# One adaLN block more in the gated mixer, unread products in TensorE's gaps, and jumps moved ahead of the last waits

## The chip, the cores and the metric

The kernel runs on one core of a Trainium2 chip. The metric is the device time of one execution in microseconds, as the median of the runs. A core has TensorE (PE in the profile, its weight loads are PEld), VectorE (DVE), ScalarE (ACT), GpSimd (POOL) and SyncE (SP). All of them take their instructions in order and wait on semaphores; DMAs go out from the queues of SP and ACT.

## The reference, cut to what matters

One inference step of a four-layer trunk for 128 context tokens and 128 latent tokens (D = 1024), everything in float32. Layer i has a token mixer and then a channel mixer (a mixture of experts):

```
for i in range(4):
    mod = silu(cond) @ w_ada[i] + b_ada[i]            # 6 x 1024: sh1, sc1, g1, sh2, sc2, g2
    h = rmsnorm(x, norm_g[i, 0]) * (1 + sc1) + sh1
    y = (hyena_mixer, gla_mixer, fnet_mixer, pool_mixer)[i](h)
    x = x + g1 * y
    h = rmsnorm(x, norm_g[i, 1]) * (1 + sc2) + sh2
    x = x + g2 * hier_moe(h, ...)                     # 16 experts, top 1 group of 4, top 2 in it
y = rmsnorm(x, final_g)
```

The shifts, scales and gates (adaLN) depend on the conditioning vectors alone, so that they can be computed at any time before they are read. `gla_mixer` is the gated linear attention (projections wq, wk, wv, wg, two chunked scans, wo); `pool_mixer` takes window means and multiplies each of four groups of channels by a 256 x 256 matrix. All weights are read once: 552 MB in all.

## The kernel before, in words

**The weight stream.** Nearly all weights come through one ring of 14 slots of 1 MB (128 partitions x 2048 floats; `RING`, `SLAB`). `piece_stream()` writes the whole order of the pieces down by hand (L119 to L146), and SP walks it: for each piece it waits until the piece that had the slot 14 places before has been multiplied, and issues the DMA (L468; the experts' pieces mostly two at a time, L459). TensorE takes the pieces in the same order. `before[i]` is what stands ahead of the experts of layer i; an expert pair has 12 pieces (three matrices of four), and a layer has 8 pairs. The four pieces of the first pair's third matrix do not use the ring but lie in the arena (`first_w2`, L427), issued ahead of the layer's other experts.

**The adaLN blocks.** w_ada is cut into 12 blocks of 8 pieces, three blocks a layer. `ada(n, lo, hi)` on TensorE (L636 to L646; the products' line is L643) multiplies pieces lo to hi - 1 of block n by the conditioning; each piece is four products in four column groups of the array. When all 8 are done, DVE copies the sums out (`ada_rows(n)`, L1391), TensorE transposes them in four products (`ada_turned(n)`, L651), and DVE adds the bias (`ada_mod(n)`, L1399, L1404), which raises `mod_ready`. Block n + 1 may begin only after that. The code spreads the blocks by hand: blocks 0 to 4 in and behind the first mixer, 5, 6 and 7 in the gated mixer, 8 behind it and in the layer's router, 9 and 10 in the third layer, and 11 in the pool mixer.

**The gated mixer** is `pe_gla`. Around the change TensorE does block 6 (L523), the four pieces of wv (L531), `ada_turned(6)`, the second gate projection (L622), and the tiles of wg (L683) among the scans.

**The pool mixer** is at the end of TensorE's program: `ada(11, 0, 2)`, `norm(6)` (L657, the sums of squares, on ACT's squares from L1108), `ada(11, 2, 5)`, the products with pool_w (L1061), which ACT copies out (L1356), `ada(11, 5, 8)`, the window means (L1068), `ada_turned(11)`, and `norm(7)`.

**The router and the experts** are `moe(i, beside)`. TensorE multiplies the router's weights and transposes h (L860, L865), subtracts the rounded half of h (L875), and, after DVE has ranked the tokens (L1528 to L1543), counts them (L881 to L885). In layers 0 to 2 pieces of the adaLN block `beside` stand between these steps; in layer 3 nothing does. Then the first tokens are gathered (L702), and the pairs begin: L737 (first and second matrix), L761 (third), L720 (scatter).

**The start.** Two small products of the implicit filter (L910, L915), `norm(0)`, the filter's third layer (L925), and its spectrum (L906), with block 0 between them. ACT issues four small DMAs first (L1097 to L1100).

**The end.** After the last norm DVE writes eight tiles of the output (L1817), each raising `out_ready`. SP stores tiles 0 to 3 after the fourth, ACT tiles 4 to 7 after the eighth; SP waits for the stores and then runs `far_rounds`. That function jumps over code for experts with more tokens than 64 (further rounds, which these inputs do not need) to the end of the program: in the code its first instruction is the jump.

Of the kernel before, what the change touches and what calls it, by code (L numbers as in the profile page):

```python
# [21 lines left out]
P = 128  # L22
# [14 lines left out]
ADAS = 3 * LAYERS  # L37
# [81 lines left out]
def piece_stream():  # L119
# [4 lines left out]
    def pieces(name, count):  # L124
# [3 lines left out]
              ada(5, 0, 5) + pieces("wq", 2) + ada(5, 5) + pieces("wk", 2) + ada(6) + pieces("wv", 4)  # L128
              + pieces("wg", 4) + ada(7) + pieces("wo", 4) + ada(8),
              ada(9) + pieces("fn", 4) + ada(10),  # L130
              ada(11, 0, 5) + pieces("pool", 1) + ada(11, 5)]
# [31 lines left out]
def build(nc, a):  # L163
# [21 lines left out]
    with ctx:  # L185
# [218 lines left out]
        def _(sp):  # L404
# [65 lines left out]
            sp.wait_ge(s("out_ready"), 4)  # L470
            sp.dma_start(a["y"][:, 0:4], hT[:, 0:4]).then_inc(s("stored"), 16)
            sp.wait_ge(s("state_stored"), 32)
            sp.wait_ge(s("stored"), 16 * 2)

# [14 lines left out]
            far_rounds(sp, "sp", reg, one_round)  # L489

# [6 lines left out]
        def pe_gla(pe, arrived, ada, ada_turned, norm, h_ready, project, residual):  # L497
# [26 lines left out]
            for c in range(4):  # L524
                w8 = arrived(("wv", c), KD)
# [9 lines left out]
            ada_turned(6)  # L535
# [3 lines left out]
            def g_tiles(first, end):  # L539

                pe.wait_ge(s("mod_ready"), 7)
# [60 lines left out]
            ada(7, 0, 3)  # L602
# [9 lines left out]
            ada(7, 3, 8)  # L612
            residual(1, "wo", oT, lambda k: pe.wait_ge(s("o_ready"), k + 1), turned=7, beside=8)
# [12 lines left out]
        def _(pe):  # L626
# [227 lines left out]

            def moe(i, beside=None):
                pe.wait_ge(s("rw_loaded"), 16 * (i + 1))
                for k in range(KD):
# [19 lines left out]
                if beside is not None:  # L877
                    ada(beside, 6, 7)
                pe.wait_ge(s("members"), i + 1)
# [6 lines left out]
                if beside is not None:  # L886
                    ada(beside, 7, 8)
                pe.wait_ge(s("htok_rest"), 4 * (i + 1))
# [19 lines left out]

            pe.wait_ge(s("filter_loaded"), 16)
            mm(bank[5][0:HY_HID, 0:L], fsmall[0:HY_EMB, 1, 0:HY_HID], fsmall[0:HY_EMB, 0, :]).then_inc(s("f_mm"), 1)  # L910
            pe.wait_ge(s("cond_ready"), 3)
# [5 lines left out]
            last.then_inc(s("f_mm"), 1)  # L917
            norm(0)
# [94 lines left out]
            moe(1, 8)  # L1013


            ada(9, 0, 2)
            norm(4)
            ada(9, 2, 5)
# [14 lines left out]
            ada(9, 5, 8)  # L1033
# [9 lines left out]
            ada_turned(9)  # L1043
            pe.wait_ge(s("mix_rows"), 8 + 4)
            residual(2, "fn", rhs=fnm, beside=10)
            moe(2, 10)
# [37 lines left out]
        def _(act):  # L1084
# [150 lines left out]
            for c in range(10):  # L1235
                spectrum(c)
# [691 lines left out]
```

## Time and profile before

| what | value |
|---|---|
| median of 3 runs (lowest, highest) | 1424.62 us (1424.25, 1424.86) |
| profiled execution, its own time | 1424.48 us |
| its span, first to last instruction | 1422.3 us |
| time outside the span | 2.2 us |
| PE busy | 1358.9 us (96%) |
| PEld, DVE, ACT, POOL busy | 748.3, 360.7, 281.8, 32.1 us |
| chain that ended last, by engine | PE 83%, DMA 13%, DVE 2%, ACT 1% |
| read from HBM | 548.98 MB, 387 GB/s over the span |
| mean granted clock of TensorE | 0.992 of 2.4 GHz |

Read the table with two resources in mind: TensorE is busy nearly all the time, and so are the DMA engines; neither alone fills the span, so that each stage has its own bound.

### The profile page before, as it was taken

Reading aid. Unit: us, or ns where it says so; the run is one execution under the profiler, and the core shown is the slowest. Engines: PE = TensorE matmul, PEld = TensorE weight load, DVE = VectorE, ACT = ScalarE, POOL = GpSimd, SP = SyncE. Lnnn points to the kernel's source line nnn. Section 1 sums busy time; section 2 is a strip of 40 time slices with the busy share of each in tenths; the row PEclk is TensorE's granted clock in tenths of the full one; section 3 lists DMA queues with packets and bytes.
Section 4 is the critical chain, followed back from the end, with each engine's and each line's share of the span. In section 5 each row is a group of like instructions: output and inputs, shape, how many; then the busy total and the mean of one; then the engine's idle time right before and its main releaser. Section 6 shows DMA issues by size and latency. Waiting matters only on the chain.

```text
span 1422.3 us, 17398 instructions
## 1 busy us (share of the span) xinstructions
PE 1358.9 (96%) x7294; PEld 748.3 (53%) x7294; DVE 360.7 (25%) x881; ACT 281.8 (20%) x511; POOL 32.1 (2%) x30
## 2 busy tenths in 40 slices
PE   7999999999989999999999989999998898999986
PEld 3786585444435788774444436744443365444433
DVE  3434514111113303323111112331111153111113
ACT  3211024111103221232111104421111053111101
POOL 0001310000000000010000000100000000000000
PEclk9999999999999999999999999999999997999999
DMA  9955999999999993499999999999999999999993
GB/s 382 420 191 214 403 416 394 428 426 428 428 425 421 421 376 102 172 413 403 429 428 426 429 423 420 421 426 428 427 427 428 424 421 425 426 428 428 427 426 153
DMA packets 55076, 552.27 MB, mean 388 GB/s; under 512 B 6033, under 2 KB 8017, under 8 KB 8913
## 3 DMA queue, kind: packets, MB, share of 16 engines
q1 hardware_dynamic: 53360, 549.09, 92.5%
q10 hardware_dynamic: 1634, 2.01, 0.4%
q8 instruction: 60, 0.98, 0.3%
q14 instruction: 22, 0.18, 0.0%
HBM read 548.98 MB, written 2.10 MB: 387 GB/s over the span
## 4 chain that ended last, share of the span: by engine, by line
PE 83%; DMA 13%; DVE 2%; ACT 1%; SPq 0%; issue 0%; POOL 0%; DVEq 0%; POOLq 0%
PE bank L737 26%; PE bank L683 14%; PE bank L761 13%; DMA ring<-in_moe_w 10%; PE bank L643 5%; PE bank L702 5%; PE bank L720 3%; PE bank L514 2%; PE bank L531 2%; DMA ring<-in_pool_w 2%; PE bank L657 2%; PE bank L968 1%; PE bank L860 1%; PE bank L593 1%; PE bank L589 1%; PE bank L744 1%
## 5 line engine op out<-in xcount | busy, mean ns | idle before, releaser
L737 PE MATMUL bank<-ring,arena 128*64 128x512 f32 x896 | 200.4, 595 | 28.1 <-DMA ring<-in_moe_w 26.5
L737 PE MATMUL bank<-ring,hT 128*64 128x512 f32 x1024 | 225.3, 594 | 0.0
L761 PE MATMUL bank<-ring,arena 128*64 128x512 f32 x896 | 198.7, 596 | 0.6 <-DMA ring<-in_moe_w 0.6
L737 PEld LDWEIGHTS bank<-ring,arena 128*64 128x64 f32 x896 | 63.7, 137 | 157.6 <-issue 131.5
L737 PEld LDWEIGHTS bank<-ring,hT 128*64 128x64 f32 x1024 | 72.1, 137 | 139.4 <-issue 137.3
L1447 DVE TENSOR_TENSOR rows<-rows,bank 128x512 f32<-128x512 f32 x32 | 22.0, 688 | 463.6 <-PE bank L737 463.6
L761 PEld LDWEIGHTS bank<-ring,arena 128*64 128x64 f32 x896 | 61.6, 137 | 117.8 <-issue 114.6
L683 PE MATMUL bank<-hT,ring 128*128 128x256 f32 x512 | 112.4, 380 | 0.0
L683 PEld LDWEIGHTS bank<-hT,ring 128*128 128x128 f32 x512 | 96.5, 190 | 15.2 <-issue 2.5
L1167 ACT ACTIVATE yv_big<-bank,arena 128x512 fp32r<-128x512 f32 x64 | 44.0, 688 | 285.5 <-PE bank L761 285.5
L1466 DVE SCALAR_TENSOR_TENSOR yv_rest<-bank,arena,yv_big 128x512 fp32r<-128x512 f32 x64 | 48.1, 751 | 200.6 <-ACT yv_big L1167 200.6
L643 PE MATMUL bank<-ring,condT 128*32 128x512 f32 x768 | 91.1, 602 | 6.6 <-DMA ring<-in_w_ada 4.9
L683 PE MATMUL bank<-arena,ring 128*128 128x256 f32 x384 | 83.8, 380 | 1.2 <-DVE arena L1659 0.9
L683 PEld LDWEIGHTS bank<-arena,ring 128*128 128x128 f32 x384 | 72.6, 190 | 12.2 <-DVE arena L1659 1.2
L702 PE MATMUL bank<-sel,htok_big 128*128 128x256 f32 x256 | 69.8, 306 | 1.7 <-DVE sel L1434 1.7
L720 PE MATMUL bank<-selT,yv_big 128*128 128x256 f32 x256 | 66.7, 297 | 1.7 <-DVE yv_rest L1466 1.7
L702 PE MATMUL bank<-sel,htok_rest 128*128 128x256 f32 x256 | 65.0, 287 | 0.0
L720 PEld LDWEIGHTS bank<-selT,yv_big 128*128 128x128 f32 x256 | 48.0, 187 | 28.5 <-issue 26.0
L702 PEld LDWEIGHTS bank<-sel,htok_big 128*128 128x128 f32 x256 | 49.8, 195 | 23.9 <-issue 20.7
L720 PE MATMUL bank<-selT,yv_rest 128*128 128x256 f32 x256 | 62.2, 279 | 0.0
L1160 ACT ACTIVATE rows<-bank 128x512 f32<-128x512 f32 x32 | 19.1, 598 | 209.4 <-PE bank L737 209.4
L1150 ACT ACTIVATE arena<-bank 128x512 f32<-128x512 f32 x32 | 19.1, 598 | 158.0 <-PE bank L702 158.0
(217 smaller groups left out, 1281.7 us busy)
## 6 DMA issues: line engine op xcount, KB each, us to landing
ring<-in_moe_w SPq DMA_DIRECT2D x152, 2048.0 KB, 20.4
ring<-in_w_ada SPq DMA_DIRECT2D x96, 1024.0 KB, 22.0
ring<-in_moe_w SPq DMA_DIRECT2D x48, 1024.0 KB, 26.8
arena<-in_moe_w SPq DMA_DIRECT2D x16, 1024.0 KB, 19.6
arena<-in_moe_w SPq DMA_DIRECT2D x8, 2048.0 KB, 11.8
ring<-in_hy_w_in SPq DMA_DIRECT2D x12, 1024.0 KB, 27.3
ring<-in_hy_w_out SPq DMA_DIRECT2D x4, 1024.0 KB, 12.3
ring<-in_gla_w_v SPq DMA_DIRECT2D x4, 1024.0 KB, 22.8
```

Of the source, the lines that this page charges most:

```text
L514: last = mm(half(4 * w + h), w8[:, k, (h % 2) * P:(h % 2) * P + P], hT[:, k].rearrange("p g t -> p (g t)"), start=k == 0, stop=k == KD - 1)
L531: last = mm(bank[b][:, 256 * (c % 2):256 * (c % 2) + 256], hT[:, k, g], w8[:, k, :], start=k == 0, stop=k == KD - 1)
L643: last = mm(ada_bank(n)[32 * j:32 * j + 32, :], condT[:, G * k:G * k + 32], w[:, j, :], start=k == 0, stop=k == KD - 1)
L657: ins = mm(bank[6][:, 0:NT], ones[:], hT[:, k].rearrange("p g t -> p (g t)"), start=k == 0, stop=k == KD - 1)
L683: last = mm(dst, w[:, k, (m % 2) * P:(m % 2) * P + P], (hT[:, k] if rhs is None else rhs[:, k]).rearrange("p g t -> p (g t)"), start=k == ...
L702: last = mm(bank[b][:, (k % 2) * NT:(k % 2) * NT + NT], htok[n % 2][:, n // 2, k * P:k * P + P], sel[:, n // 2].rearrange("p e j n -> p (e ...
L720: last = mm(half(m), part[:, m * P:m * P + P], selT[:], start=first_pair and m % 2 == 0 and part is yv[0], stop=False, skip_group_check=True)
L737: last = mm(bank[4 + kind][SLOTS * e:SLOTS * e + SLOTS, :], x[:, k, at:at + SLOTS], w[:, kk, e, :], start=k == 0, stop=k == KD - 1)
L761: last = mm(bank[6 + q // 2][SLOTS * e:SLOTS * e + SLOTS, :], hidT[:, f, SLOTS * e:SLOTS * e + SLOTS], w[:, ff, e, :], start=f == 0, stop= ...
L1167: act_fn(yv[0][:, 512 * h:512 * h + 512], bank[6 + h][:], ACT.Identity, scale=wcol) \
L1447: tt(sil[:], sil[:], bank[5][:], ALU.mult).then_inc(s(pre + "hid_ready"), 1)
L1466: stt(yv[1][:, cols], bank[6 + h][:], wcol, yv[0][:, cols].bitcast(F32), ALU.mult, ALU.subtract) \
```

## The change

The order of the stream and of TensorE's blocks: layer 1 takes block 7 between the second and the third piece of wv, and blocks 8 and 9 where 7 and 8 were; layer 2 takes 10 and 11; layer 3 none. DVE's calls follow. `keep_running(n, x, b)` multiplies ones by x into a bank and nobody reads it; `wide_ones` is a column of ones repeated 512 times. Three of ACT's first DMAs are issued after the first norm. The output goes in four stores instead of two, and `far_rounds` comes ahead of the last waits on SP and ACT.

```diff
     before = [ada(0) + pieces("w_in", 12) + ada(1) + ada(2) + ada(3) + pieces("w_out", 4) + ada(4),
-              ada(5, 0, 5) + pieces("wq", 2) + ada(5, 5) + pieces("wk", 2) + ada(6) + pieces("wv", 4)
-              + pieces("wg", 4) + ada(7) + pieces("wo", 4) + ada(8),
-              ada(9) + pieces("fn", 4) + ada(10),
-              ada(11, 0, 5) + pieces("pool", 1) + ada(11, 5)]
+              ada(5, 0, 5) + pieces("wq", 2) + ada(5, 5) + pieces("wk", 2) + ada(6) + pieces("wv", 2) + ada(7)
+              + pieces("wv", 4)[2:] + pieces("wg", 4) + ada(8) + pieces("wo", 4) + ada(9),
+              ada(10) + pieces("fn", 4) + ada(11),
+              pieces("pool", 1)]
...
-            sp.wait_ge(s("out_ready"), 4)
-            sp.dma_start(a["y"][:, 0:4], hT[:, 0:4]).then_inc(s("stored"), 16)
-            sp.wait_ge(s("state_stored"), 32)
-            sp.wait_ge(s("stored"), 16 * 2)
...
             far_rounds(sp, "sp", reg, one_round)
+            sp.wait_ge(s("state_stored"), 32)
+            for k in (0, 4):
+                sp.wait_ge(s("out_ready"), k + 2)
+                sp.dma_start(a["y"][:, k:k + 2], hT[:, k:k + 2]).then_inc(s("stored"), 16)
+            sp.wait_ge(s("stored"), 16 * 4)
...
             for c in range(4):
+                if c == 1:
+                    ada_turned(6)
+                if c == 2:
+                    ada(7, 0, 8)
                 w8 = arrived(("wv", c), KD)
...
-            ada_turned(6)
+            ada_turned(7)
             gates(pe, 1)
...
-                pe.wait_ge(s("mod_ready"), 7)
+                pe.wait_ge(s("mod_ready"), 8)
...
-            ada(7, 0, 3)
+            ada(8, 0, 3)
...
-            ada(7, 3, 8)
-            residual(1, "wo", oT, lambda k: pe.wait_ge(s("o_ready"), k + 1), turned=7, beside=8)
+            ada(8, 3, 8)
+            residual(1, "wo", oT, lambda k: pe.wait_ge(s("o_ready"), k + 1), turned=8, beside=9)
...
+            wide_ones = ones[:, 0:1].broadcast_to([P, 512])
+            def keep_running(times, x, b=7):
+                for _ in range(times):
+                    mm(bank[b][:, 0:x.shape[1]], ones[:], x)
...
             def moe(i, beside=None):
                 pe.wait_ge(s("rw_loaded"), 16 * (i + 1))
+                if beside is None:
+                    pe.wait_ge(s("mod_ready"), ADAS)
+                    keep_running(2, wide_ones)
...
                 if beside is not None:
                     ada(beside, 6, 7)
+                else:
+                    keep_running(3, wide_ones)
                 pe.wait_ge(s("members"), i + 1)
...
                 if beside is not None:
                     ada(beside, 7, 8)
+                else:
+                    keep_running(1, wide_ones)
...
+            pe.wait_ge(s("cond_ready"), 1)
+            keep_running(2, ones[:], 0)
             pe.wait_ge(s("filter_loaded"), 16)
             mm(bank[5][0:HY_HID, 0:L], ...).then_inc(s("f_mm"), 1)
+            keep_running(12, ones[:], 0)
...
             last.then_inc(s("f_mm"), 1)
+            keep_running(3, ones[:], 0)
             norm(0)
...
-            ada(11, 0, 2)
             norm(6)
-            ada(11, 2, 5)
+            keep_running(2, wide_ones)
             pw = arrived(("pool", 0), KD)
...
-            ada(11, 5, 8)
             pe.wait_ge(s("mix_rows"), 12 + 4)
...
-            ada_turned(11)
             norm(7)
             moe(3)
...
-            act.dma_start(base[:], a["c_base"]).then_inc(s("base_loaded"), 16)
-            act.dma_start(ar(19472, 3 * P), a["c_masks"]).then_inc(s("masks_loaded"), 16)
             act.dma_start(skip_row[0:1], a["skip"]).then_inc(s("skip_loaded"), 16)
-            act.dma_start(rw[:], a["router"][0]).then_inc(s("rw_loaded"), 16)
...
             inverse_root(0)
+            act.dma_start(base[:], a["c_base"]).then_inc(s("base_loaded"), 16)
+            act.dma_start(ar(19472, 3 * P), a["c_masks"]).then_inc(s("masks_loaded"), 16)
+            act.dma_start(rw[:], a["router"][0]).then_inc(s("rw_loaded"), 16)
...
-            act.wait_ge(s("out_ready"), 8)
-            act.dma_start(a["y"][:, 4:8], hT[:, 4:8]).then_inc(s("stored"), 16)
             far_rounds(act, "act", reg, one_round)
+            for k in (2, 6):
+                act.wait_ge(s("out_ready"), k + 2)
+                act.dma_start(a["y"][:, k:k + 2], hT[:, k:k + 2]).then_inc(s("stored"), 16)
...
-            ada_rows(6)
-            ada_mod(6)
+            for n in (6, 7):
+                ada_rows(n)
+                ada_mod(n)
```

The other lines of the diff put 10 for 9, 11 for 10 and so on in the third layer, and take block 11's calls out of DVE's pool mixer.

## Rows read from the trace of the kernel before

**Rows 1.** The page's second part: what the DMAs moved in 40 slices of 35.6 us

```profile
GB/s 382 420 191 214 403 416 394 428 426 428 428 425 421 421 376 102 172 413 403 429 428 426 429 423 420 421 426 428 427 427 428 424 421 425 426 428 428 427 426 153
```

**Rows 2.** Windows: stretch, length, busy time (instructions) by engine, clock, DMA share, GB/s

```profile
524.00:590.00 66.00, 64.62 (x388) 57.08 (x387) 21.92 (x35) 17.77 (x26) 0.00 (x0) 1.00 0.30 108
1240.00:1329.00 89.00, 89.00 (x460) 37.64 (x456) 14.99 (x24) 10.89 (x17) 0.00 (x0) 1.00 1.01 428
```

**Rows 3.** TensorE's waits from 1326 to 1407 us: total, times, longest

```profile
PE bank L737 <- DMA ring<-in_moe_w: 7.5, 6, 1.3
```

**Rows 4.** The gated mixer: chain of waits, then SP's issues and their landing

```profile
488.59 7.00 PE bank L643 x64
495.59 27.82 PE bank L531 x128
...
469.73 3.07 SPq L468 DMA_DIRECT2D ring<-in_gla_w_v  x4
...
ring<-in_gla_w_v SPq DMA_DIRECT2D x4, 1024.0 KB, 22.8
```

**Rows 5.** TensorE's timeline in the pool mixer and router, then two chain pieces

```profile
1149.38 3.72 PE L657 MATMUL bank<-hT,ones 128*128 128x256 f32 x16
1156.25 7.17 PE L1061 MATMUL bank<-ring,hT 128*128 128x256 f32 x32 [0.44 <-DMA ring<-in_pool_w]
1163.35 2.78 PE L643 MATMUL bank<-ring,condT 128*32 128x512 f32 x24
1166.07 3.84 PE L1068 MATMUL bank<-cm,arena 128*128 128x128 f32 x32
1170.18 3.62 PE L657 MATMUL bank<-hT,ones 128*128 128x256 f32 x16
1176.08 0.59 PE L860 MATMUL bank<-rw,hT 128*128 128x20 f32 x4 [2.28 <-DVE hT L1415]
...
1189.96 6.00 PE bank L702 x32
1195.96 13.88 PE bank L737 x64
```

**Rows 6.** ACT's and DVE's timelines in the same stretch

```profile
1146.88 4.03 ACT L1108 ACTIVATE hT<-xT 128x256 f32<-128x256 f32 x8
1163.46 0.60 ACT L1356 ACTIVATE arena<-bank 128x512 f32<-128x512 f32 x1 [1.13 <-PE bank L1061]
...
1184.24 0.17 DVE L1528 TENSOR_REDUCE arena<-bank 128x2 f32<-128x8 f32 x1 [4.50 <-PE bank L860]
```

**Rows 7.** A window inside layer 3's router

```profile
1180.00:1185.00 5.00, 5.00 (x27) 4.83 (x25) 0.66 (x5) 1.39 (x3) 0.00 (x0) 0.50 1.01 416
```

**Rows 8.** The same steps in layer 1's router: timeline, then the chain

```profile
635.26 0.62 PE L860 MATMUL bank<-rw,hT 128*128 128x20 f32 x4
640.24 0.17 DVE L1528 TENSOR_REDUCE arena<-bank 128x2 f32<-128x8 f32 x1 [1.73 <-PE bank L860]
...
645.94 4.06 PE bank L702 x32
```

**Rows 9.** The start: TensorE's timeline, the chain, a DMA's landing, a group

```profile
11.99 6.06 PE L657 MATMUL bank<-hT,ones 128*128 128x256 f32 x16 [0.45 <-ACT hT L1108]
...
2.50 9.00 DMA xT<-in_x
26.77 3.63 PE bank L906 x8
...
arena<-in_c_window SPq DMA_DIRECT2D x1, 512.0 KB, 13.8
...
L1620 DVE TENSOR_TENSOR arena<-bank,arena 128x512 f32<-128x512 f32 x8 | 5.2, 680 | 4.6 <-PE bank L925 4.5
```

**Rows 10.** The end: ACT's last issue and the stores' landing

```profile
1415.42 0.35 ACTq L1366 DMA_DIRECT2D out_y<-hT  x1
...
out_y<-hT ACTq DMA_DIRECT2D x1, 512.0 KB, 4.1
```

More of the change, by code:

```diff
@@ L1012, in _ @@
             pe_gla(pe, arrived, ada, ada_turned, norm, h_ready, project, residual)
-            moe(1, 8)
-            ada(9, 0, 2)
+            moe(1, 9)
+            ada(10, 0, 2)
             norm(4)
-            ada(9, 2, 5)
+            ada(10, 2, 5)
             pe.wait_ge(s("cm_loaded"), 16 * 2)
@@ L1032, in _ @@
                     last.then_inc(s("mix_mm"), 1)
-            ada(9, 5, 8)
+            ada(10, 5, 8)
             pe.wait_ge(s("mix_rows"), 8)
@@ L1042, in _ @@
                     last.then_inc(s("mix_mm"), 1)
-            ada_turned(9)
+            ada_turned(10)
             pe.wait_ge(s("mix_rows"), 8 + 4)
-            residual(2, "fn", rhs=fnm, beside=10)
-            moe(2, 10)
-            ada(11, 0, 2)
+            residual(2, "fn", rhs=fnm, beside=11)
+            moe(2, 11)
             norm(6)
-            ada(11, 2, 5)
+            keep_running(2, wide_ones)
             pw = arrived(("pool", 0), KD)
@@ L1788, in _ @@
                 tt(o, o, ors[:, m // 2], ALU.mult).then_inc(s("o_ready"), 1)
-            ada_rows(7)
+            ada_rows(8)
             residual(1, g1(1))
-            ada_mod(7)
-            moe(1, 8)
+            ada_mod(8)
+            moe(1, 9)
             norm(4)
-            ada_rows(9)
+            ada_rows(10)
             residual(2, g1(2))
-            ada_mod(9)
-            moe(2, 10)
+            ada_mod(10)
+            moe(2, 11)
             norm(6)
@@ L1804, in _ @@
             chain(tt(xT[:], xT[:], gb.unsqueeze(3).broadcast_to([P, KD, G, L]), ALU.add))
-            ada_rows(11)
             for m in range(KD):
@@ L1811, in _ @@
                 last.then_inc(s("x_added"), 1)
-            ada_mod(11)
             moe(3)
```

## The prediction, made before the changed kernel was run

> **What bounds the kernel now.** I read three views in turn. First the page's slices: from slice 18 on the DMAs move 400 to 429 GB/s in each slice but the last, and two stretches are low, slices 3 and 4 (the first mixer) and 16 and 17 (the gated mixer) [rows 1]. Then windows: in the gated mixer, 524 to 590 us, TensorE is busy for 64.62 of 66 us while the DMAs are busy for 0.30 of it, at 108 GB/s; in the last experts both are full, at 428 GB/s [rows 2]. A piece of 1.049 MB thus takes 2.45 us. Then TensorE's waits: at the very end it waits 7.5 us in six steps for experts' weights [rows 3]. So the gated mixer is bound by TensorE with a full ring, and from there on the transfers never rest; whatever weights lie behind that point are paid for at 2.45 us each, if TensorE is not later itself. The first three layers' end stretches keep their waits: nothing in the change takes pieces from between them.
>
> **Block by block.** *The gated mixer, TensorE.* It gets 8 pieces more. Block 6 took 7.00 us [rows 4], and four transposes more cost about 0.4 (the gap between the window means' end, 1169.8, and the next norm at 1170.18 [rows 5]): +7.4 us, with nothing beside it, since TensorE is the bound. Do the pieces come in time? The four issues of wv span 469.7 to 472.8 us and land in 22.8 us at the median [rows 4]; at one piece in 2.45 us that puts the first at about 490 and the second at 492.7. Block 7 then lands from 495 to 512, the third piece of wv at 515. TensorE gets through block 6 at 495.6, and each piece of wv takes 27.82 / 4 = 7.0 us [rows 4]: block 7 is wanted from 510 to 516 and the third piece at 517. So there are 2 us to spare at the tightest place, and I take 0 for waiting (bounds 0 and 2). The turned sums of block 6 are now wanted at 502.6 instead of 523; behind that wait stand wv's remaining pieces and block 7. DVE copies them out when block 6 ends and TensorE works on the first piece of wv for 7 us meanwhile, so nothing.
>
> *The gated mixer, transfers.* The ring stays full there before and after, so that the transfers restart when TensorE frees the same slots, 7.4 us later. Layers 1 and 2 are moved by 7.4 us as a whole: ahead of their experts stands the same number of pieces between full ring and experts.
>
> *The pool mixer and the last router* (times in the frame of before, the 7.4 left out). Sums of squares started at 1149.38 behind two pieces of block 11 and ended at 1153.1 [rows 5]; ACT's squares end at 1150.9 [rows 6], so that the last product can end at 1151.3: 1.8 us earlier. The pool products waited for their weights until 1156.25; with five pieces of block 11 gone ahead of them these land 12 us earlier, and the products gain 1.9. The last copy of their result ended at 1163.46 + 0.60 = 1164.1, the window means began at 1166.07 behind three more pieces [rows 5, 6]: another 2.0. Without the transposes the next norm comes 0.2 earlier still: 4.1 us. Two unread products of 512 columns take 1.8 us (four such took 3.63 [rows 9]) and lie in the wait of 2.28 us ahead of L860 [rows 5]. The router itself ran at half clock: 0.50, the 1.2 GHz level, from 1180 to 1185 [rows 7]; the engine had waited 2.28 us just before and then made only short products. From L860 to DVE's first step it took 8.16 us against 4.98 in layer 1, and the first gather 6.00 against 4.06 [rows 5, 6, 8]. At full clock that gives 3.2 and 1.9 back. Three unread products end about when DVE has the members (they take 2.7 us of the 5.7 between L1528 and the gather [rows 8]), and the one behind them lies beside DVE's selection: at nothing, bounds 0 and 1. Sum: the last experts begin 4.1 + 3.2 + 1.9 = 9.2 us earlier, at 1186.8.
>
> *The last experts.* Two limits. TensorE's own: 9.2 plus the waits of 7.5 that go if the weights are there: 16.7. The transfers': before, behind the pool weights (landed 1156.2) came 3 pieces of block 11, 4 in the arena and 92 in the ring: 99 x 2.45 gives 1398.8. Now the pool weights land at 1143.9, and 4 + 14 pieces later, at 1188.0, the ring is full. TensorE frees two slots at 1186.8 + 2 x 1.74 = 1190.3 (8 pieces take 13.88 [rows 5]), and a new transfer needs about 2 us to run, so the transfers stand still for 4 us; then 78 x 2.45 gives 1383.1, 15.7 earlier. The smaller counts: 15.7 us, so that about 1 us of waiting stays, and of the 19.6 us of transfers that the block cost, 4 are lost again.
>
> *The start.* Sixteen products of `norm(0)` took 6.06 us, the same sixteen 3.6 to 3.7 elsewhere [rows 5, 9]: for the most part half clock. With unread products from 2.5 us on it should run full by 11 us: 2.4 us, and x, which lands at 11.5 after 9.00, may gain up to 1 us from 0.4 MB of ACT's loads that now come later. But DVE's products with the window can't begin before it lands (issued near 4, 13.8 on the way: 17.8, perhaps 1 us sooner); eight of them at 0.68 and a step of about 1 us for the skip row stand ahead of the spectrum [rows 9], which then starts at 23.3 to 24.3 instead of 26.77, 2.5 to 3.5 sooner. I take 2.7 us (bounds 0.5 and 3.5); it carries through, as TensorE is the bound until well into the first mixer, where the ring is full. The unread products ahead of the first piece of block 0 stand where TensorE has nothing else.
>
> *The end.* The last store was issued at 1415.42 and landed 4.1 us later [rows 10]; half as many bytes save 0.6. Then 2.8 us remain to 1422.3, in which SP's last wait is over and its jump comes; with the jump ahead, between 0 and 2.8 go: I take 1.4. No row prices a jump. Sum 2.0 (bounds 0.6 and 3.4). SP's wait for the states is long past then.
>
> **Sum.** + 7.4 - 15.7 - 2.7 - 2.0 = -13.0 us, on the profiled execution's 1424.48 (span 1422.3 and 2.2 around it, 0.1 under the median): 1411.5 us.
>
> **A rule that speaks against it.** The clock has to hold through L860 and L865, 4.9 us in which half of the products are transposes. In layer 1, with three adaLN pieces ahead and two behind (7.00 / 8 = 0.88 us each [rows 4], 2.6 and 1.8 us), those steps ran at full speed [rows 8]; in layer 3 the clock fell [rows 7]. The Trainium skill, page "TensorE: Matmul & The Clock Gate", part 4 (PE-mode transpose), says that transposes do not count as activity as products do. By that rule the two unread products ahead are too few, and the sum would be that of the first rival; by the row of layer 1 it is mine.
>
> **Rivals.**
> *1. The clock still falls in the last router.* For it: the fillers ahead of it are 1.8 us where layer 1 has 2.6, and nothing fills the wait behind L865. Then 3.2 and 1.9 stay lost, the experts begin at 1191.9, the full ring stands from 1188.0 to about 1197.4, 9.4 us, and the transfers end 10.3 earlier instead of 15.7 (TensorE's limit 11.6): 7.4 - 10.3 - 4.7 = -7.6, 1416.9 us.
> *2. The lead of the transfers is lost wholly in the ring*, so that the last waits of 7.5 us stay: slots are freed two at a time and the standstill becomes 10 us or more. Against it: 18 pieces of lead and 1.74 us a piece. Then only 9.2 counts: 7.4 - 9.2 - 4.7 = -6.5, 1418.0 us.
> *3. Start and end give nothing*, for the clock rises no sooner and the jump was no cost: 7.4 - 15.7 = -8.3, 1416.2 us.
> *4. Slower: the clock falls already in the pool mixer*, since block 11's products no longer fill it. The point that decides is the norm at 1151: it is paced by ACT's squares, and 1.8 us of unread products follow. At 1.2 GHz L1061 takes 13.8 instead of 7.17, L1068 about 6.9 instead of 3.84, L657 6.9 instead of 3.62, together 13 us, and the router's 5.1 stay. The experts then begin 13 - 4.1 = 8.9 later, the transfers stand still for 22 us and end 2.5 us later than before: 2.5 + 7.4 - 4.7 = +5.2, 1429.7 us. Against it: TensorE's gaps there stay under 1 us.
>
> **Chances.** Mine 0.62; first rival 0.18; second 0.06; third 0.08; fourth 0.04; 0.02 for other losses. The range, from the bounds: the start between 0.5 and 3.5 and the end between 0.6 and 3.4 alone give 1409.3 to 1415.1 around mine, the first rival reaches 1416.9. I give 1408.0 to 1417.5. A change within 0.2% (2.8 us) can't be told from none; only the fourth rival and part of the rest lie outside "faster": faster 0.93, same 0.03, slower 0.04.
>
> **What would show it.** The gated mixer from the end of block 5 to the first experts 7.4 us longer, with no wait of TensorE for weights in wv. The clock 1.00 from 1150 to 1200 and the router's first step 5 us behind L860. From the last norm of layer 2 to the last experts' first product 9.2 us less. In the last experts a dip of the transfers of some 4 us near their start, and at most 2 us of waits for weights. The first mixer's w_in products from about 40 instead of 42.7 us. About 1 us from the last store's landing to the end. The prediction fails if the last waits stay, if the granted clock shows 0.5 in the last layer, or if TensorE waits for block 7 or wv.

## The result, and the profile after

| | median (lowest to highest), us | runs |
|---|---|---|
| kernel before | 1424.74 (1424.25 to 1425.24) | 4 |
| changed kernel | 1414.22 (1412.42 to 1415.23) | 4 |

The ratio is 0.9923, with a 95% interval from 0.9909 to 0.9938: 10.5 us (0.8%) less, where 13.0 were forecast. The profiled execution of the changed kernel is its longest run, 1415.23 us with a span of 1412.9.

The page's GB/s row, 40 slices of 35.3 us. Where [rows 1] has 376, 102 and 172 in slices 15 to 17 (the gated mixer), there are now 421, 260 and 120; and slice 34 is a new dip, 320.

```profile
GB/s 383 420 206 223 404 406 407 428 427 428 427 424 421 421 421 260 120 420 408 415 428 426 429 424 421 420 425 428 428 428 425 428 420 320 405 426 429 427 427 205
```

The gated mixer: first the window (length, busy time and instructions by engine, clock, DMA share, GB/s), which carried 108 GB/s before [rows 2]; then the chain, with block 7's products and the first experts of layer 1.

```profile
524.00:590.00 66.00, 64.63 (x381) 57.12 (x380) 20.06 (x31) 18.91 (x27) 0.00 (x0) 1.00 0.56 218
```

```profile
506.83 7.00 PE bank L647 x64
...
650.35 4.05 PE bank L706 x32
654.84 5.29 PE bank L741 x23
```

The pool mixer and the last router, TensorE's timeline and two pieces of the chain; they answer to [rows 5, 6]. L661 is the norm, L864 the unread products, L1082 the pool products, L1088 the window means, L874 the router, L706 the first gather, L741 the first experts' products.

```profile
1153.48 4.23 PE L661 MATMUL bank<-hT,ones 128*128 128x256 f32 x16
1157.56 1.89 PE L864 MATMUL bank<-ones 128*128 128x512 f32 x4
1159.92 8.06 PE L1082 MATMUL bank<-ring,hT 128*128 128x256 f32 x32 [0.48 <-DVE hT L1435]
1168.67 3.84 PE L1088 MATMUL bank<-cm,arena 128*128 128x128 f32 x32 [0.69 <-ACT arena L1375]
1172.34 3.62 PE L661 MATMUL bank<-hT,ones 128*128 128x256 f32 x16
1175.80 1.89 PE L864 MATMUL bank<-ones 128*128 128x512 f32 x4
1178.12 0.59 PE L874 MATMUL bank<-rw,hT 128*128 128x20 f32 x4 [0.43 <-DVE hT L1435]
...
1188.76 4.06 PE bank L706 x32
1192.82 13.88 PE bank L741 x64
```

Windows around the beginning of the last experts: the clock is full, the transfers are not.

```profile
1185.00:1190.00 5.00, 4.78 (x23) 2.45 (x22) 4.01 (x23) 1.46 (x5) 0.00 (x0) 1.00 0.74 308
1190.00:1195.00 5.00, 5.00 (x36) 3.44 (x36) 2.30 (x8) 3.66 (x5) 0.00 (x0) 1.00 0.13 56
1195.00:1200.00 5.00, 5.00 (x26) 1.67 (x24) 0.00 (x0) 0.12 (x1) 0.00 (x0) 1.00 0.52 154
1200.00:1205.00 5.00, 5.00 (x26) 1.72 (x24) 0.00 (x0) 0.48 (x1) 0.00 (x0) 1.00 1.02 436
```

TensorE's waits from 1326 to 1401 us, 7.5 us in six before [rows 3]:

```profile
PE bank L741 <- DMA ring<-in_moe_w: 4.9, 4, 1.3
```

The start: the first norm (timeline), the spectrum and the w_in products (chain). The norm took 6.06 us before and the spectrum began at 26.77 [rows 9].

```profile
11.95 3.62 PE L661 MATMUL bank<-hT,ones 128*128 128x256 f32 x16
...
24.29 3.63 PE bank L924 x8
...
40.24 4.79 PE bank L687 x17
```

The end: the last norm's products in the chain, and ACT's stores (4.1 us to landing before [rows 10]).

```profile
1400.68 4.12 PE bank L661 x16
...
out_y<-hT ACTq DMA_DIRECT2D x2, 256.0 KB, 3.2
```

Read one behind the other, the chain's times of the two kernels (for the end of layer 2's experts the timeline's) give the balance of the spans (1422.3 and 1412.9):

| point | before | after | difference | step |
|---|---|---|---|---|
| end of layer 0 | 443.56 | 440.42 | -3.1 | -3.1 |
| first experts of layer 1 | 650.44 | 654.84 | +4.4 | +7.5 |
| end of layer 2's experts | 1147.53 | 1153.48 | +6.0 | +1.6 |
| first experts of layer 3 | 1195.96 | 1192.82 | -3.1 | -9.1 |
| last norm | 1407.04 | 1400.68 | -6.4 | -3.2 |
| end of the span | 1422.3 | 1412.9 | -9.4 | -3.0 |

### The profile page after: what moved, and what is told of

Its sections match the earlier page's. It is cut to its first block, busy times and chain, and to the rows that moved or that the text cites. A ratio compares the mean times of both kernels' runs of the same rounds, so it can differ in the third digit from the quotient of the medians.

```text
span 1412.9 us, 17502 instructions
## 1 busy us (share of the span) xinstructions
PE 1364.8 (97%) x7344; PEld 748.9 (53%) x7344; DVE 360.5 (26%) x881; ACT 281.8 (20%) x511; POOL 32.1 (2%) x30
## 4 chain that ended last, share of the span: by engine, by line
PE 86%; DMA 11%; DVE 2%; ACT 1%; issue 0%; POOL 0%; DVEq 0%; SPq 0%; POOLq 0%
PE bank L741 27%; PE bank L687 14%; PE bank L765 13%; DMA ring<-in_moe_w 11%; PE bank L647 5%; PE bank L706 4%; PE bank L724 4%; PE bank L535 2%; PE bank L514 2%; PE bank L661 2%; PE bank L990 1%; PE bank L874 1%; PE bank L748 1%; PE bank L597 1%; PE bank L593 1%; PE bank L924 1%
## 5 line engine op out<-in xcount | busy, mean ns | idle before, releaser
L741 PE MATMUL bank<-ring,hT 128*64 128x512 f32 x1024 | 225.5, 594 | 0.3 <-DMA ring<-in_moe_w 0.3
L741 PE MATMUL bank<-ring,arena 128*64 128x512 f32 x896 | 200.1, 595 | 26.4 <-DMA ring<-in_moe_w 25.1
L765 PE MATMUL bank<-ring,arena 128*64 128x512 f32 x896 | 198.6, 596 | 0.0
L741 PEld LDWEIGHTS bank<-ring,arena 128*64 128x64 f32 x896 | 63.7, 137 | 155.6 <-issue 130.2
L741 PEld LDWEIGHTS bank<-ring,hT 128*64 128x64 f32 x1024 | 72.0, 137 | 139.9 <-issue 136.4
L765 PEld LDWEIGHTS bank<-ring,arena 128*64 128x64 f32 x896 | 61.4, 137 | 117.1 <-issue 113.8
L687 PEld LDWEIGHTS bank<-arena,ring 128*128 128x128 f32 x384 | 72.6, 190 | 12.2 <-DVE arena L1679 1.2
L706 PE MATMUL bank<-sel,htok_big 128*128 128x256 f32 x256 | 68.0, 301 | 0.8 <-DVE sel L1454 0.8
L706 PE MATMUL bank<-sel,htok_rest 128*128 128x256 f32 x256 | 63.3, 282 | 0.0
L706 PEld LDWEIGHTS bank<-sel,htok_big 128*128 128x128 f32 x256 | 48.3, 189 | 23.7 <-issue 20.5
L1176 ACT ACTIVATE rows<-bank 128x512 f32<-128x512 f32 x32 | 19.1, 598 | 209.3 <-PE bank L741 209.3
```

The source lines that it names most:

```text
L687: last = mm(dst, w[:, k, (m % 2) * P:(m % 2) * P + P], (hT[:, k] if rhs is None else rhs[:, k]).rearrange("p g t -> p (g t)"), start=k == ...
L706: last = mm(bank[b][:, (k % 2) * NT:(k % 2) * NT + NT], htok[n % 2][:, n // 2, k * P:k * P + P], sel[:, n // 2].rearrange("p e j n -> p (e ...
L741: last = mm(bank[4 + kind][SLOTS * e:SLOTS * e + SLOTS, :], x[:, k, at:at + SLOTS], w[:, kk, e, :], start=k == 0, stop=k == KD - 1)
L765: last = mm(bank[6 + q // 2][SLOTS * e:SLOTS * e + SLOTS, :], hidT[:, f, SLOTS * e:SLOTS * e + SLOTS], w[:, ff, e, :], start=f == 0, stop= ...
```

## The experiments

Each ran in five rounds beside the kernel before. Its median in the three sets was 1424.73, 1424.99 and 1425.19 us; "gain" is the difference of medians within a set.

| run | median (lowest to highest), us | gain | ratio to before, 95% |
|---|---|---|---|
| changed kernel again | 1414.00 (1412.02 to 1415.45) | 10.7 | 0.9919 [0.9905, 0.9932] |
| move only | 1424.76 (1422.93 to 1427.19) | 0.0 | 0.9998 [0.9989, 1.0007] |
| no late fill | 1419.22 (1417.18 to 1420.51) | 5.5 | 0.9963 [0.9949, 0.9976] |
| move and late fill | 1419.91 (1418.43 to 1424.05) | 5.3 | 0.9965 [0.9953, 0.9977] |
| start only | 1421.46 (1420.34 to 1422.24) | 3.5 | 0.9976 [0.9967, 0.9985] |
| start, products only | 1422.27 (1421.22 to 1423.39) | 2.9 | 0.9976 [0.9965, 0.9987] |
| end only | 1421.94 (1419.49 to 1424.03) | 3.1 | 0.9975 [0.9966, 0.9984] |
| jump only | 1422.58 (1421.30 to 1425.01) | 2.4 | 0.9986 [0.9977, 0.9995] |
| four spare pieces | 1416.76 (1414.72 to 1418.16) | 8.2 | 0.9943 [0.9930, 0.9957] |
| block in halves | 1411.04 (1409.26 to 1411.61) | 13.7 | 0.9905 [0.9890, 0.9920] |
| a quarter left | 1409.30 (1407.71 to 1412.78) | 15.9 | 0.9889 [0.9874, 0.9903] |

**1. The move alone.** The blocks move; the unread products, the late DMAs, the four stores and the early jumps are taken out.

```diff
-            keep_running(2, wide_ones)        # and every other keep_running
...
+            act.dma_start(rw[:], a["router"][0]).then_inc(s("rw_loaded"), 16)   # early, as before
```

> Only the move of the blocks (block 7 into wv, 8 to 11 a place ahead, none in the pool mixer): no unread products anywhere, first DMAs and end as before. My theory: the ring is full when the last experts begin, so that a lead of the transfers is worth only as much as TensorE's own start there. Gated mixer + 7.4 us; pool mixer - 4.1; the router stays at half clock, so nothing more there, and the full ring stands some 14 us instead of 9: the transfers' end comes about 2 us later than in the kernel before, 1424 to 1427 us. Rival (what counts is the bytes behind the gated mixer, 19.6 us of transfers gone against 7.4 added): 1424.6 + 7.4 - 12 to - 19.6 = 1412 to 1419 us.

It gained nothing. TensorE's last experts begin 3 us later than before, and the transfers stand still in front of them. Chain (the last experts' first products and the last norm) and windows of this run, and the same windows of the kernel before:

```profile
1198.94 13.88 PE bank L741 x64
...
1406.00 4.08 PE bank L661 x16
...
1180.00:1200.00 20.00, 16.16 (x95) 14.29 (x97) 12.21 (x55) 10.73 (x23) 0.00 (x0) 0.66 0.60 254
1200.00:1220.00 20.00, 20.00 (x104) 8.27 (x102) 2.14 (x4) 3.35 (x5) 0.00 (x0) 1.00 0.78 315
```

```profile
1180.00:1200.00 20.00, 16.80 (x86) 12.93 (x86) 7.95 (x40) 7.82 (x15) 0.00 (x0) 0.64 1.02 427
1200.00:1220.00 20.00, 20.00 (x104) 8.21 (x102) 2.89 (x5) 2.81 (x5) 0.00 (x0) 1.00 1.00 423
```

The last number of each row is GB/s. Against the kernel before, (427 + 423 - 254 - 315) x 20 / 428 = 13.1 us of transfers are missing here, about what the transfers had gained in the gated mixer: summed over windows of 20 us, this run was 12.8 us ahead of the kernel before at 1180 and 0.4 behind at 1220. Both kernels show the low clock (0.64 and 0.66); in the kernel before the transfers go on beneath it. From the last experts' first product to the last norm (L661) it takes 207.1 us here and 211.1 before: 3.0 us later at the beginning, 1.0 earlier at the last norm. What that constant means is taken up behind the last experiment.

**2. Without the late unread products**, the changed kernel otherwise.

```diff
             norm(6)
-            keep_running(2, wide_ones)
...
-                    keep_running(3, wide_ones)   # router: 2 ahead, 3 and 1 behind
```

> The changed kernel without the unread products in the pool mixer and in the last router; start and end stay. My theory: the granted clock falls to 0.50 in the last router as it did before, 3.2 us from L874 to DVE's first step and 1.9 in the first gather are lost, and since the ring is full by then the whole 5.1 us reach the end: 1414.2 + 5.1 = 1419.3 us. Rival 1 (the transfers hide it): 1414.2. Rival 2 (the clock falls already in the pool mixer, from 1158 us on): another 8 to 13 us, 1427 or more.

As mine: 5.2 us less gained than with them (10.7 and 5.5), where the first rival of the prediction stood 5.4 above its forecast. A window of the router, then the chain:

```profile
1180.00:1185.00 5.00, 5.00 (x26) 4.97 (x26) 1.37 (x7) 2.04 (x5) 0.00 (x0) 0.50 1.00 423
...
1190.07 5.43 PE bank L706 x32
1195.51 13.88 PE bank L741 x64
```

From the norm at 1151.48 to the experts it takes 44.0 us, against 39.3 in the changed kernel: 1.0 of it in the pool products (9.09 against 8.06), 2.2 from the router to the gather, 1.4 in the gather. That 1.0 is the fourth rival of the prediction in small: the clock was 0.91 and 0.75 from 1155 to 1165, where the changed kernel's is 1.00. The windows from 1180 to 1220 show 199 and 369 GB/s: 13.2 us of transfers missing.

**3. The move with the late unread products**, start and end as before.

```diff
-            keep_running(12, ones[:], 0)      # start: none of the three
...
+            act.wait_ge(s("out_ready"), 8)    # end: two stores ahead of the jumps
```

> The changed kernel with the start and the end of the kernel before: the blocks' move, and the unread products of the pool mixer and the last router (2, 2, 3 and 1). The move alone gave nothing, the start alone 3.5 and the end alone 3.1 us. Mine: the move is worth something only with these products, since without them TensorE's clock falls in the last router and the transfers stand still longer; the whole change's 10.6 less 3.5 and 3.1 leaves 4.0: 1420.8 us, between 1419.5 and 1422. Rival: start and move help each other (the earlier stream of transfers is what the move lacks), the products of the router do little by themselves: 1424.0 or more.

As mine: the move is worth 0.0 us without these products and 5.3 with them, and start (3.5), end (3.1) and this (5.3) make 11.9 for the whole's 10.6, which their intervals of about 1.3 us each allow. So nothing in the start is needed for the move to pay. From 1180 to 1220 the transfers move 287 and 385 GB/s: 8.3 us missing.

**4. The changed kernel again.** No edit.

> The changed kernel again, beside the others on the same chip, as the mark for them: 1412.4 to 1415.3 us, and again 8 to 9 us in which the transfers stand still near 1190.

The same time as expected, but another course: 11.3 us of transfers are missing from 1180 to 1220 (227 and 382 GB/s), where 8 to 9 were expected, and in this execution the clock fell in the router in spite of the unread products.

```profile
1180.00:1185.00 5.00, 5.00 (x23) 4.46 (x22) 1.88 (x12) 2.88 (x8) 0.00 (x0) 0.50 1.00 423
...
1193.90 13.88 PE bank L741 x64
```

From the norm (at 1151.98 here, 1153.48 in the first profile) to the experts it takes 41.9 us in place of 39.3; the last norm comes at 1401.04 against 1400.68. So one execution of this kernel differs from another by 1.5 us at the beginning of layer 3, and by whether the clock falls. Over all profiles the unread products do hold it more often than not: of the six profiles with two of them ahead of the last router (the changed kernel's two, move and late fill, four spare pieces, halves, a quarter left) five show 1.00 all through that router, and the seven profiles without them (before, move only, no late fill, the two of the start, end only, jump only) all show 0.50 in a part of it.

**5. The start alone.**

```diff
+            keep_running(2, ones[:], 0)       # and 12 and 3 further on
...
             inverse_root(0)
+            act.dma_start(base[:], a["c_base"]).then_inc(s("base_loaded"), 16)   # and masks, router
```

> The kernel before with nothing but the start of the change: 17 unread products (2, 12 and 3) in TensorE's gaps of layer 0's beginning, and ScalarE's three transfers (base, masks, router) issued behind its first inverse root. Mine: the 12 blocked microseconds at the beginning end 2.5 earlier, as they do in the whole change, and as layers 0 to 3 are bound by TensorE or by transfers whose whole stream starts earlier with it, the 2.5 reach the end: 1422.2 us, between 1421.5 and 1423.0. Rival: the last experts are bound by the transfers, whose stream is held by nothing at the start (the ring is full there), so the start's gain is eaten as more waiting for slabs: 1424.7.

**6. The start's products alone**, the three DMAs where they were.

```diff
+            keep_running(2, ones[:], 0)       # and 12 and 3 further on
```

> As the run with the start alone, but ScalarE's three transfers stay where they were: only the 17 unread products. Mine: what the start gains is the shorter time of the first norm's products (3.5 in place of 6.1 us) and of what follows at the higher clock, and the products alone bring it: 1421.5 to 1422.5 us, first product of the input projection near 40.3. Rival: the three transfers, issued ahead of ScalarE's first squares, are what holds layer 0's beginning: 1424 or more, first product near 42.5.

Both as mine (the first 0.04 us below its range). The rival of the first, that the gain is lost as more waiting in the last experts, fell: the waits there are 6.1 us in place of 7.5. The first w_in products begin at 39.81 us with products and DMAs and at 40.63 with the products alone (42.72 before); the chains:

```profile
23.87 3.63 PE bank L913 x8
...
39.81 5.22 PE bank L683 x19
```

```profile
24.68 3.63 PE bank L913 x8
...
40.63 4.57 PE bank L683 x16
```

The 0.8 us between them is what the later DMAs may bring; but the changed kernel, with products and DMAs, stands at 40.24, in the middle, and the ratios don't tell the two apart. The 2.9 us that the start alone gains at the w_in products are still there at the last norm (1403.94, 3.1 below before).

**7. The end alone.**

```diff
+            far_rounds(sp, "sp", reg, one_round)
             sp.wait_ge(s("state_stored"), 32)
+            for k in (0, 4):                  # and (2, 6) on ACT, behind its far_rounds
+                sp.wait_ge(s("out_ready"), k + 2)
```

> The kernel before with nothing but the end of the change: the branch to the further rounds stands ahead of the last waits on SP and ScalarE, and the output goes out in four stores in place of two. Mine: the time from the last norm's products to the end of the program falls from 15.3 to 12.2 us, as in the whole change: 1421.6 us. By the sum of the prediction (0.6 for the stores, 1.4 for the branch): 1422.7. Rival: the branch's code comes in beside the last layer's work anyway and only the stores count: 1424.1.

**8. The jump alone**, still two stores.

```diff
+            far_rounds(act, "act", reg, one_round)
             act.wait_ge(s("out_ready"), 8)
             act.dma_start(a["y"][:, 4:8], hT[:, 4:8]).then_inc(s("stored"), 16)
-            far_rounds(act, "act", reg, one_round)
```

> As the run with the end alone, but the output still goes out in two stores: only the branch stands ahead of the last waits. By the sum of the prediction 1.4 us less than before: 1423.3. If the 3.0 us of the end are mostly the branch's: 1422.2, with the last store's issue following the last wait at once. Rival (stores only): 1424.7.

The end alone came out 0.3 above the 1421.6 expected, the jump alone at 1422.6, nearer to 1422.2 (the branch's gain) than to the 1423.3 of the prediction's sum. From the last norm's products to the end of the span it takes 15.3 us before (1407.04 to 1422.3), 12.2 in the changed kernel, 12.1 with the whole end (1407.68 to 1419.8) and 12.4 with the jump alone:

```profile
1409.12 4.08 PE bank L656 x16
...
core 0: 1421.5 us, clock 0.992
```

So by the profiles the jump is worth 2.9 us and the stores 0.3, where the prediction's price for the jump was 1.4; by the medians it is 2.4 and 0.7, and the interval of the jump's ratio reaches from 0.7 to 3.3 us. Which of the two engines' jumps it is, no run tells. What the last 4 us hold is seen in the DMA view, GB/s in 40 slices: first before, from 1419 to 1423, then the jump alone, from 1418 to 1422.

```profile
GB/s 0 0 0 0 0 0 0 0 0 0 0 0 0 0 82 0 0 0 0 0 0 0 0 0 0 0 0 0 0 0 0 0 0 0 0 0 0 0 82 0
q14 instruction: 2, 0.02, 1.0%
```

```profile
GB/s 0 41 0 451 369 328 492 287 451 492 328 410 410 328 492 287 123 41 41 82 41 41 0 41 41 0 0 0 0 0 0 0 0 0 0 0 0 0 0 0
q14 instruction: 1, 0.01, 0.5%
```

Before, the output had landed at 1419.5; behind it two loads of instructions are seen, at 1420.4 and at 1422.8 (this one behind the span's end at 1422.3), and one small packet. With the jump ahead of the last waits the one load lies ahead of 1420, and the store's last packets are the last thing that moves. The price is measured; that it is the loading of the code behind the jump is argued from these rows, not shown. The Trainium skill, page "Runtime: NRT & Kernel Launch", section "Instruction fetch mechanics", says that a taken branch whose target is outside the loaded window waits for a fetch; the rows above fit that, with 2.4 to 2.9 us, but whether this target lay outside no run shows. Its page "Advanced Engine Details and Errata", section "Control Flow Timing", gives about 51 ns for a branch, which isn't what this one costs.

**9. Four spare pieces.** The changed kernel with four more pieces of 1 MB in front of the pool weights, awaited and not read.

```diff
-              pieces("pool", 1)]
+              pieces("spare", 4) + pieces("pool", 1)]
...
+            for c in range(4):
+                arrived(("spare", c), KD)
```

> The changed kernel with four more pieces of the size of an adaLN piece (1 MB each, 2.45 us each at 428 GB/s, 9.8 us together) sent through the ring ahead of the pool mixer's piece and read by nothing; TensorE only waits for their arrival. Mine: in the changed kernel the transfers stand still for some 9 us at 1186 to 1203 because the ring is full, so bytes that pass the ring before that are nearly free: the standstill goes, the last experts begin where they did, and the time rises by 0 to 2 us: 1414.0 to 1416.2. Rival: the last experts are bound by the sum of the bytes, wherever they lie: 1414.1 plus 9.8, 1423.9.

Near mine, 0.6 above its range, and 7.1 below the rival: 9.8 us more of transfers cost 2.6 us (1416.76 against 1414.1, the middle of the changed kernel's two medians). The dip is gone:

```profile
1180.00:1200.00 20.00, 19.67 (x123) 12.34 (x123) 10.86 (x51) 10.33 (x20) 0.00 (x0) 1.00 0.99 412
1200.00:1220.00 20.00, 20.00 (x104) 8.22 (x102) 3.64 (x6) 3.17 (x5) 0.00 (x0) 1.00 0.97 403
```

1.6 us are missing here, 10.7 in the changed kernel (236 and 386 GB/s). So bytes in front of the full ring cost about a quarter of their time. But it isn't the length of the standstill that sets the end: here it is nearly gone, the last experts begin where they do in the changed kernel's second execution (1193.96 and 1193.90), and the last norm comes 2.2 us later (1403.27 and 1401.04).

**10. The last block in halves.** Pieces 0 to 3 of block 11 stay in layer 2, 4 to 7 go to the pool mixer; VectorE adds the two sums (one transpose group and one set of copies more). In layer 2's router unread products stand for the four missing pieces; in the pool mixer two of the pieces stand where its two unread products were.

```diff
-              ada(10) + pieces("fn", 4) + ada(11),
-              pieces("pool", 1)]
+              ada(10) + pieces("fn", 4) + ada(11, 0, 4),
+              ada(11, 4, 6) + pieces("pool", 1) + ada(11, 6)]
...
+            ada_turned(12)
```

> The changed kernel with block 11 in two halves: pieces 0 to 3 in the third layer, pieces 4 to 7 in the pool mixer (two in place of its two unread products, two behind the pool products), summed by DVE in two steps; unread products in a bank of their own stand for the four pieces in layer 2's router. My theory (the transfers stand still 9 us with a full ring ahead of the last experts): layer 2's experts have their weights 9.8 us earlier and lose most of their 10 us of waits, the pool mixer takes 1.2 + 0.4 us more of TensorE, the last experts begin some 8 us earlier, before the ring is full, and there is no standstill: 1414.2 - 7 to - 9 = 1405 to 1407 us. Rival (the standstill costs nothing, the same bytes end at the same time): 1414 to 1416 us.

Right in direction, 3.0 us where 7 to 9 were expected. The last experts begin at 1184.70, 8.1 earlier, and the transfers never stand in front of them:

```profile
1180.00:1200.00 20.00, 19.78 (x110) 9.86 (x109) 4.63 (x17) 4.50 (x7) 0.00 (x0) 1.00 1.01 428
```

But 3.5 us of them went missing earlier, at the beginning of layer 2's experts (first product at 936.72), whose ring now filled too soon: 352 GB/s from 940 to 960, where the changed kernel has 428.

**11. A quarter of it left to the pool mixer**: pieces 6 and 7. Unread products stand for them in layer 2's router; those of the pool mixer stay.

```diff
+              ada(10) + pieces("fn", 4) + ada(11, 0, 6),
+              pieces("pool", 1) + ada(11, 6)]
```

> The changed kernel with pieces 6 and 7 of the last adaLN block (2 of 8, where the run in halves had 4) left to the pool mixer, their sum added on VectorE to that of pieces 0 to 5. In the run in halves the transfers lost 3.6 us near 950 that the changed kernel doesn't lose, and none of the 9 to 11 at 1186 to 1203. Mine: with two pieces the loss near 950 is under 2 us and the standstill before the last experts is 4 to 6 us, so that the transfers' lead at 1220 to 1360 is about what it was in halves (5 to 7 us over the changed kernel's): 1411.0, between 1410 and 1412.5. Rival: the standstill is not a matter of how many bytes are ahead of the experts but of when their first products release the slots; it stays at 9 us or more until 4 pieces fill it, and the time is the changed kernel's, 1414.

The rival fell (5.1 us are missing from 1180 to 1220, not 9), and the time came out 1.7 below mine, 0.7 below its range. Nothing is missing from 940 to 960 (422 GB/s), and half of the standstill is gone:

```profile
1180.00:1200.00 20.00, 19.78 (x103) 9.28 (x103) 6.18 (x30) 5.57 (x10) 0.00 (x0) 1.00 0.87 355
1200.00:1220.00 20.00, 20.00 (x109) 9.25 (x106) 3.63 (x6) 3.17 (x5) 0.00 (x0) 1.00 0.95 386
...
1187.68 13.88 PE bank L743 x64
...
1394.80 4.12 PE bank L663 x16
```

The last experts begin at 1187.68 and the last norm at 1394.80, 5.9 before the changed kernel's. At 1409.30 us it beats both kernels; the halves' interval overlaps its own.

**The profiles side by side.** Times from the chain; "missing" is what the transfers moved less from 1180 to 1220 than in the kernel before, in us of the full rate.

| run | missing | last experts' first product | last norm | between |
|---|---|---|---|---|
| changed kernel, first profile | 10.7 | 1192.82 | 1400.68 | 207.9 |
| changed kernel again | 11.3 | 1193.90 | 1401.04 | 207.1 |
| move only | 13.1 | 1198.94 | 1406.00 | 207.1 |
| no late fill | 13.2 | 1195.51 | 1402.71 | 207.2 |
| move and late fill | 8.3 | 1194.26 | 1401.29 | 207.0 |
| a quarter left | 5.1 | 1187.68 | 1394.80 | 207.1 |
| four spare pieces | 1.6 | 1193.96 | 1403.27 | 209.3 |
| block in halves | 0 | 1184.70 | 1394.75 | 210.1 |
| before | 0 | 1195.96 | 1407.04 | 211.1 |

In the first six the transfers stood, and the last norm comes 207 us behind the last experts' first product whether 5 or 13 us are missing. What went missing ahead of that product makes no difference: the end follows TensorE's start, as the expectation of the move alone had it. In the last three the transfers hardly stood there; the waits for weights from 1326 to 1401 are longer in them (6.0, 5.6 and 7.5 us against 4.0 to 4.9), and so it is the transfers that set the end. So the quarter gains because its last experts begin 5.1 us earlier (6.2 against the second execution), not because the gap is smaller. About 3 us of that are fewer waits in layer 2's experts, whose weights now have two pieces less ahead of them: 5.8 us, against 8.9 and 8.7 in the changed kernel's two profiles. Where the rest comes from no run takes apart.

## Why the prediction was right in its sum and wrong in two of its terms

The time came out 2.7 us above the 1411.5 forecast and inside the range. By itself it doesn't speak for the forecast: the sums of the first and the third rival (1416.9 and 1416.2) lie as near, at 2.7 and 2.0 us. The balance by stages does. That the sum came so near is luck in part, for start and end gave 1.4 us more than forecast and the last experts 3.3 less.

- **The gated mixer**, +7.4: +7.5, with no wait of TensorE for weights in wv. Right.
- **Layers 1 and 2 moved as a whole**: +1.6 instead of 0. The second execution of the same kernel began layer 3 at 1151.98 in place of 1153.48, so that 1.5 of this can be the execution's and not the change's.
- **The pool mixer and the last router**, -9.2: -9.1 in the first profile. The unread products carry about half of it: without them the stretch from the norm is 4.7 us longer. The first rival happened, too, in the second profile. The worked-out price of a fallen clock, 5.4 us, was measured as 5.2 and 5.3 with the products taken out; where the clock falls in spite of them, for a shorter time, the stretch is 2.6 longer. The Trainium skill's rule on transposes (page "TensorE: Matmul & The Clock Gate", part 4) is not decided by this: with the same two products ahead of the router the clock held in one execution and not in the other, and in five of six profiles in all.
- **The last experts**, -6.5 beyond their earlier start: -3.2. **This is the term that was mis-sized**: "then 78 x 2.45", which takes the transfers to run without a break once they have started again. Place and cause of the first standstill were right: the last slot had landed at 1194.3, TensorE freed the first two at 1196.3 (1192.82 + 3.5), SP issued at 1196.49, and 4.2 us of transfers were lost between 1194 and 1200, as worked out. But SP got through only three issues of 2 MB, 14.7 us of transfers, before it stood again:

```profile
1156.15 47.53 SPq L459 DMA_DIRECT2D ring<-in_moe_w  x6
1213.09 0.33 SPq L449 DMA_DIRECT2D arena<-in_moe_w  x1
...
SPq L449 <- PE bank L765: 12.5, 2, 9.4
...
1212.00:1214.00 2.00, 2.00 (x12) 0.72 (x10) 0.02 (x1) 0.69 (x1) 0.00 (x0) 1.00 0.44 188
1214.00:1216.00 2.00, 2.00 (x12) 0.69 (x10) 0.73 (x1) 0.00 (x0) 0.00 (x0) 1.00 0.88 233
```

Next in its order is a place in the arena that the first pair's third matrix (L765) still holds. SP waits for it for 9.4 us, until 1213.09, and the transfers run out at 1212: 2.0 us lost. In the kernel before SP waits there for 9.4 us too, but with more transfers queued (434 and 418 GB/s from 1212 to 1216). The prediction's last experts take 211.1 - 6.5 = 204.6 us; five executions with a full ring took 207.0 to 207.2 and the first profile 207.9. Of the 2.5 us between, 2.0 are this second gap; the other 0.5, and the 0.7 that the first profile has on top, stay open.

Another loss is seen that the prediction didn't have, and it cost nothing: from 1186 on the rate fell, before the ring was full (windows of 2 us: 328, 229, 115 and 25 GB/s, so 100 + 199 + 313 + 403, x 2 / 428 = 4.7 us). All slots had landed by 1194.3 all the same, before the first of them was freed again, and the table of the profiles shows the end to be the same with 5.1 and with 13.2 us missing.

- **The last waits**, at most 2 us: 4.9, and 4.0 to 4.2 in the other five executions with a full ring. They stay since the transfers run 2.5 us later behind TensorE's start than worked out; the sign announced for a failure was seen.
- **The start**, -2.7: 2.5 at the w_in products, 3.1 at the layer's end, and 3.5 with the start alone. Right; with the products alone it is 2.9, and what the later DMAs add (0.6 by the medians, 0.8 by the chains) isn't told from nothing.
- **The end**, -2.0: -3.0. The split was off both ways: by the profiles the stores gave 0.3 instead of 0.6, the jump 2.9 instead of 1.4. The upper bound of 2.8 for the jump was the better value to take: no other work in the trace lay in that time.

By the profiled executions 3.6 us of the 13.0 are missing: 3.3 in the last experts and 1.6 ahead of layer 3, less 1.0 at the end and 0.4 at the start.

## What to carry to other kernels

Weights moved ahead of a bottleneck buy time only as far as the ring can hold them: ask at each later stage whether the ring fills before TensorE begins to free it. If it does, that stage's end hangs on TensorE's first product there (207 us behind it in all such profiles), a longer lead of the transfers is worth nothing more, and the length of the gap is no measure of the loss. Then see whether a few pieces left behind let TensorE come to that stage sooner (two pieces here, worth 5.2 us, as much as the move with its fillers). When the transfers restart, follow the issuing engine's order further on: its next wait can open a second gap, which the full queue had hidden. A gap's fillers and a moved block may be worth nothing one without the other, so price them together. Put jumps ahead of the last wait.

## What the runs showed of the hardware that was not expected

- As the queue of transfers runs dry, the rate falls over some 8 us: 328, 229, 115 and 25 GB/s in windows of 2 us. It cost nothing here, since all had landed before TensorE freed the next slots. The Trainium skill, page "DMA: Bandwidth & Descriptors", section "Two DMAs through the same engine are not ordered", says that nothing orders DMAs across the 16 engines; the trace fits it in that the DMA share falls from window to window, 0.79, 0.54, 0.27 and 0.06, as if the engines finished one by one. That reading is argued, not shown.
- A jump behind the last wait costs 2.4 us by the medians and 2.9 by the profiles.
- The granted clock in the same stretch of the same kernel was 1.00 in one execution and 0.50 in another (the 2.4 and the 1.2 GHz level); what decides between them no run here tells.
